# Pairwise attention: the order of scores and transposes, one sequence for two kinds of attention, and a mask on another engine

## What is computed

```
# even layer (block 0), 8 heads: banded, with a sink in the denominator
p = exp(q k / 8 + bias - m)  for keys 0..127 back ; o = p / (sum p + exp(sink - m)) v
# even layer, 8 heads: stick-breaking, strictly causal
z = q k / 8 ;  log_keep = log_sigmoid(-z) where key < query, else 0
a = exp(log_sigmoid(z) + sum of log_keep of later keys) where key < query, else 0 ;  o = a v
# odd layer (block 1), 16 heads: softmax, causal, a bias that stands for three dilated patterns
# block 2, 16 query heads on 4 key heads: softmax over the keys an index has chosen
```

## Time and profile before

| | us |
|---|---|
| median of 3 runs | 3341.68 |
| lowest and highest | 3340.91, 3341.93 |
| the profiled execution | 3343.73 |
| its span in the profile | 3341.9 |

### The profile page before, as it was taken

One profiled execution on the slowest core, in us unless ns is written; L12 is line 12 of the kernel. 1 busy time (PEld: TensorE's weight loads), 2 busy tenths in 40 slices (PEclk: granted clock), 3 DMA queues, 4 the chain that ended last, 5 costly groups with the idle time before them and its releaser, 6 DMA issues.

```text
span 3341.9 us, 36935 instructions
## 1 busy us (share of the span) xinstructions
PE 3184.2 (95%) x14548; PEld 2576.1 (77%) x14548; DVE 1413.5 (42%) x2242; ACT 1188.2 (36%) x1999; POOL 223.0 (7%) x441
## 2 busy tenths in 40 slices
PE   8999995999999999999988999999999998989998
PEld 7888884777788888887866877888887775768887
DVE  3332336554333233323455543332325876443322
ACT  3322326443332132222345533322225636332221
POOL 1000100010000000000310100000042100010000
PEclk9999997999999999999999999999989999989999
DMA  4332220231332323322322412233222230223332
GB/s 142 95 96 100 89 89 1 89 126 51 93 92 93 107 89 95 100 96 83 94 83 70 139 50 87 92 99 101 68 89 76 76 102 19 82 76 95 95 101 70
DMA packets 212606, 291.44 MB, mean 87 GB/s; under 512 B 13873, under 2 KB 135985, under 8 KB 212305
## 3 DMA queue, kind: packets, MB, share of 16 engines
q1 hardware_dynamic: 209792, 279.59, 26.6%
q0 software_dynamic: 2640, 9.50, 0.9%
HBM read 286.94 MB, written 2.10 MB: 86 GB/s over the span
## 4 chain that ended last, share of the span: by engine, by line
PE 86%; DVE 6%; ACT 5%; POOL 1%; issue 1%; DMA 0%; POOLq 0%; DVEq 0%; ACTq 0%
PE ps L94 83%; PE ps L97 3%; DVE sxP L112 1%; DVE ebQ L115 1%; ACT sxP L100 1%; ACT ocP L100 1%; DVE ocP L112 1%; ACT L100 0%; DVE hTl L109 0%; DVE ebP L103 0%; ACT xn L100 0%; POOL stat L103 0%; ACT hTh L100 0%; ACT wh L100 0%; DVE s_ri L115 0%
## 5 line engine op out<-in xcount | busy, mean ns | idle before, releaser
L103 DVE TENSOR_TENSOR wl<-raw,wh 128x1024 fp32r<-128x1024 f32 (+1 forms) x530 | 640.9, 1216 | 1247.5 <-ACT wh L100 1242.6
L100 ACT ACTIVATE wh<-raw 128x1024 fp32r<-128x1024 f32 (+1 forms) x530 | 552.5, 1051 | 1360.0 <-PE ps L94 1316.2
L94 PE MATMUL ps<-hTh,wh 128*128 128x512 f32 x2144 | 839.7, 392 | 16.6 <-DVE hTl L109 16.6
L94 PE MATMUL ps<-hTl,wh 128*128 128x512 f32 x2144 | 837.2, 390 | 0.0
L94 PE MATMUL ps<-hTh,wl 128*128 128x512 f32 x2144 | 837.0, 390 | 0.0
L94 PEld LDWEIGHTS ps<-hTh,wh 128*128 128x128 f32 x2144 | 404.3, 189 | 104.2 <-DVE hTl L109 13.7
L94 PEld LDWEIGHTS ps<-hTl,wh 128*128 128x128 f32 x2144 | 404.2, 189 | 84.9 <-issue 1.0
L94 PEld LDWEIGHTS ps<-hTh,wl 128*128 128x128 f32 x2144 | 404.3, 189 | 84.2
L94 PE MATMUL ps<-wh,hTh 128*128 128x512 f32 (+2 forms) x832 | 324.5, 390 | 10.3 <-DVE hTl L109 5.8
L94 PE MATMUL ps<-wl,hTh 128*128 128x512 f32 (+2 forms) x832 | 321.2, 386 | 0.0
L94 PE MATMUL ps<-wh,hTl 128*128 128x512 f32 (+2 forms) x832 | 321.2, 386 | 0.0
(11 more groups left out here) (344 smaller groups left out, 3918.9 us busy)
## 6 DMA issues: line engine op xcount, KB each, us to landing
raw<-in_ffn_w_gu SPq DMA_DIRECT2D x352, 256.0 KB, 3.1
raw<-in_ffn_w_down SPq DMA_DIRECT2D x88, 512.0 KB, 3.5
raw<-in_xa_w_kv SPq DMA_DIRECT2D x32, 512.0 KB, 3.9
raw<-in_w_in SPq DMA_DIRECT2D x32, 512.0 KB, 3.7
raw<-in_od_w_in SPq DMA_DIRECT2D x24, 512.0 KB, 3.6
raw<-in_w_ffn_gate SPq DMA_DIRECT2D x44, 256.0 KB, 2.9
raw<-in_w_ffn_up SPq DMA_DIRECT2D x44, 256.0 KB, 3.1
raw<-in_w_ffn_down SPq DMA_DIRECT2D x22, 512.0 KB, 3.8
```

Source lines behind the costliest of these rows:

```text
L94: return self.made(lambda e: e.matmul(*a, **k))
L100: return self.made(lambda e: e.activation(*a, **k))
L103: return self.made(lambda e: e.tensor_tensor(*a, **k))
```

## The change

- A `Stage` takes the place of the pairs' tiles: it holds a sequence of pairs that may be of different kinds. The even layer's banded and stick-breaking pairs are one such sequence of eight (`EV`), with no handover and no drain between them.
- Row tiles are five slots, handed to the heads in turn; a head waits for the transposes of the head five before it. The fifth slot is in memory that is free during the stage.
- On PE, the next pair's first two score groups are issued between the transposes of the even and the odd head, and the third group after the odd head's. A banded pair has only two groups, so all its scores go first.
- Stick-breaking: DVE's addition of the mask in the score bank is gone. POOL runs two `affine_select`s for each block after the sigmoids, on the last 128 columns of `P` (fill 0) and of `Q` (fill 1), and DVE's scan waits for `masked`. The `Q` tiles are three, handed to the heads in turn. The scan's second operand is one zero column, broadcast. The memsets are of single columns, and POOL does them before the stage.
- ACT and POOL wait, ahead of the even stage, for tiles of the projection to be free (`even_wait`), and DVE for one ahead of the odd stage; all were used long before.

The diff, cut to its core:

```diff
...
+    class Stage:
+
+
+
+
+        def __init__(self, tag, parts, slots, pt, small, keeps=None):
+            self.tag, self.seq = tag, [(A, s) for A in parts for s in range(A.N)]
+            self.N = len(self.seq)
+            self.p = [(sb(f"{tag}Pa{j}", [P, 512], F32, a), sb(f"{tag}Pb{j}", [P, 768], F32, b))
+                      for j, (a, b) in enumerate(slots)]
             self.pt = [sb(f"{tag}PT{u}", [P, NT, S], F32, pt) for u in range(2)]
             self.sm = [sb(f"{tag}sm{b}", [P, 5, 8], F32, small) for b in range(2)]
...
+        def sbank(self, g, n, u):
+            return 2 * ((self.sfirst[g] + n) % 2) + u
+        def tbank(self, g, u, n):
+            return 4 + (self.tfirst[g] + u * len(self.seq[g][0].groups) + n) % 3
+        def scores(self, g, n, u):
+            A, at = self.seq[g][0], 0
+            for i in A.groups[n]:
+                W = A.spans[i][3]
+                yield i, W, bank[self.sbank(g, n, u)][:, at:at + W]
+        def row(self, g, u, i):
+            pa, pb = self.p[(2 * g + u) % 5]
+            W, o = self.seq[g][0].spans[i][3], (0, 128, 384, 0)[i]
+            return (pa if i == 3 else pb)[:, o:o + W]
+        def keep(self, g, u, i, skip=0):
+            _, _, o, W = CAUSAL[i]
+            return self.q[(2 * g + u) % 3][:, o + i + skip:o + i + skip + W]
+        def slot_wait(self, e, g, u):
+            j = 2 * g + u - 5
+            if j >= 0:
+                e.wait_ge(turned, (self.tag, j // 2, len(self.seq[j // 2][0].groups) - 1, j % 2))
...
-        scores(0)
-        for s in range(A.N + 2):
-            if s >= 2:
-                values(s - 2)
-            if 1 <= s <= A.N:
-                turn(s - 1, 0)
-                turn(s - 1, 1)
-            if s + 1 < A.N:
-                scores(s + 1)
...
+        scores(0, slice(None))
+        for g in range(T_.N + 2):
+            if g >= 2:
+                values(g - 2)
+            if 1 <= g <= T_.N:
+                turn(g - 1, 0)
+            if g + 1 < T_.N:
+                scores(g + 1, slice(0, 2))
+            if 1 <= g <= T_.N:
+                turn(g - 1, 1)
+            if g + 1 < T_.N:
+                scores(g + 1, slice(2, 3))
...
+        def sigmoids(g):
+            A, s = T_.seq[g]
+            act.wait_ge(ones_set, tag)
+            for n in range(len(A.groups)):
+                for u in range(2):
+                    act.wait_ge(scored, (tag, g, n, u))
+                    T_.slot_wait(act, g, u)
+                    j = 2 * g + u - 3
+                    if T_.seq[j // 2][0].stick:
+                        act.wait_ge(normed, (tag, j // 2, j % 2, A.groups[-1][-1]))
+                    for i, W, src in T_.scores(g, n, u):
+                        act.activation(T_.row(g, u, i), src, AF.Sigmoid)
+                        act.activation(T_.keep(g, u, i), src, AF.Sigmoid, scale=-1.0).then_inc(expd, (tag, g, u, i)).also(
+                            drained, (tag, g, "s", n, u))
...
+    def pool_stage(pool, T_):
+
+        tag = T_.tag
+        for g, (A, _) in enumerate(T_.seq):
+            if A.stick:
+                for group in A.groups:
+                    for u in range(2):
+                        for i in group:
+                            W = A.spans[i][3]
+                            pool.wait_ge(expd, (tag, g, u, i))
+                            for t_, fill in ((T_.row(g, u, i), 0.0), (T_.keep(g, u, i), 1.0)):
+                                dg = t_[:, W - P:W]
+                                ins = pool.affine_select(out=dg, in_=dg, compare_op=ALU.is_ge, fill=fill, base=-1,
+                                                         pattern=[[-1, P]], channel_multiplier=1)
+                            ins.then_inc(masked, (tag, g, u, i))
...
-        def before(s):
-
-            dve.wait_ge(const_in, 0)
-            for n, group in enumerate(A.groups):
-                for u in range(2):
-                    dve.wait_ge(scored, (A.tag, s, n, u))
-                    for i, W, src in A.scores(s, n, u):
-                        ins = dve.tensor_tensor(src[:, W - P:W], src[:, W - P:W], mis("strict"), ALU.add)
-                    ins.then_inc(maxed, (A.tag, s, n, u))
...
+        def breaks(g, u):
+            A, _ = T_.seq[g]
             for group in A.groups:
                 for i in group:
                     W = A.spans[i][3]
+                    rev = T_.keep(g, u, i)[:, ::-1]
+                    dve.wait_ge(masked, (tag, g, u, i))
+                    dve.tensor_tensor_scan(rev, rev, T_.zero[:, 0:1].to_broadcast([P, W]), 1.0, ALU.mult, ALU.add).then_inc(step, (tag, g, u, i))
+                    dve.wait_ge(step, (tag, g, u, i))
+                    dve.tensor_tensor(T_.row(g, u, i), T_.row(g, u, i), T_.keep(g, u, i, 1), ALU.mult).then_inc(
+                        normed, (tag, g, u, i))
...
+        def end(g, u):
+            (breaks if T_.seq[g][0].stick else later)(g, u)
+        first(0)
+        for g in range(T_.N + 2):
+            if g < T_.N:
+                end(g, 0)
+            if g >= 2:
+                A, s = T_.seq[g - 2]
+                dve.wait_ge(valued, (tag, g - 2))
+                dve_lo(dve, bank[VBANK][:, :], A.O, A.base + s, slice(0, S)).also(drained, (tag, "o", g - 2))
+            if g + 1 < T_.N and not T_.seq[g + 1][0].stick:
+                first(g + 1)
+            if g < T_.N:
+                end(g, 1)
...
-    def pe_even(pe):
-        pe_pairs(pe, EA, qaT, kaT, lambda s: ("in0", 0, "T", s), lambda c: ("in0", 1, "T", c), lambda s: s // 2,
-                 lambda h, kt: e_tk[:, kt, 128 + 64 * (h // 4):192 + 64 * (h // 4)], [("in0", 1, t) for t in range(NT)])
-        handover(pe, "stick")
-        pe_pairs(pe, EB, qbT, kbT, lambda s: ("qb", s), lambda c: ("kb", c), lambda s: s,
-                 lambda h, kt: e_vb[:, kt, 64 * h:64 * h + 64], [("vb", t) for t in range(NT)])
-
-    def act_even(act):
-        act_pairs(act, EA, hT("out0"), 0, "in0")
-        handover(act, "stick")
-        act_pairs(act, EB, hT("out0"), 4, "in0")
-
-    def dve_even(dve):
-        def bias(h, i, W):
-            dve.wait_ge(table_in, "evb")
-            return evb[:, 256 * (h + 1) - W:256 * (h + 1)]
-        dve_pairs(dve, EA, hT("out0"), 0, bias)
-        handover(dve, "stick")
-        dve_pairs(dve, EB, hT("out0"), 4)
+    def even_wait(e):
+
+        for b in range(2):
+            e.wait_ge(xn_gone, ("in0:1", b))
+        for g in range(2):
+            e.wait_ge(tmp_gone, ("in0", g))
 
     def pool_even(pool):
-        handover(pool, "stick")
-        pool.memset(EB.zr[:, :], 0.0).then_inc(step, "eb zero")
-        for b in range(2):
-            for u in range(2):
-                pool.memset(EB.q[b][u][:, :], 1.0).then_inc(ones_set, "eb")
+        even_wait(pool)
+        pool.memset(EV.zero[:, :], 0.0)
+        for t_ in EV.q:
+            for i, (_, _, o, W) in enumerate(CAUSAL):
+                pool.memset(t_[:, o + i + W:o + i + W + 1], 1.0).then_inc(ones_set, "ev")
+        pool_stage(pool, EV)
...
+    EV = Stage("ev", [EA, EB], [(ev, ev)] * 4 + [(ev_xn, ev)], ev, ev, [ev_gone, ev_gone, ev_xn])
+               [(od, od)] * 4 + [(od_gone, od_gone)], od, od)
+               [(sx_p, sx_p), (sx_p, sx_p), (sx_sc, sx_sc), (sx_xn, sx_xn), (sx_p, sx_xn)], Area(a1 + 16384), sx_p)
...
```

More of the change, by code:

```diff
@@ L746, in row @@
[L746 to L752, removed]
-    VBANK = 7
[L756 to L760, removed]
-            pe.wait_ge(put, kkey(kb))
-            for n, group in enumerate(A.groups):
+            if keeps:
+                self.q = [sb(f"{tag}Q{j}", [P, CAUSAL_W + NT], F32, a) for j, a in enumerate(keeps)]
+                self.zero = sb(f"{tag}Z", [P, 1], F32, small)
@@ new lines, in slot_wait, with pe_stage, scores @@
+        def slot_wait(self, e, g, u):
+            j = 2 * g + u - 5
+            if j >= 0:
+                e.wait_ge(turned, (self.tag, j // 2, len(self.seq[j // 2][0].groups) - 1, j % 2))
+    VBANK = 7
+    def pe_stage(pe, T_):
+        tag = T_.tag
+        def scores(g, part):
+            A, s = T_.seq[g]
+            kb = A.kv_of(s)
+            pe.wait_ge(put, A.qkey(s))
+            pe.wait_ge(put, A.kkey(kb))
+            for n in range(len(A.groups))[part]:
+                group = A.groups[n]
@@ L763, in scores @@
                 for u in range(2):
[L764 removed]
+                    b = T_.sbank(g, n, u)
                     pe.wait_ge(drained, pe.held[b])
[L766 to L768 removed]
+                    pe.held[b] = (tag, g, "s", n, u)
+                for both in zip(T_.scores(g, n, 0), T_.scores(g, n, 1)):
                     for u, (i, W, dst) in enumerate(both):
@@ new lines, in copies @@
+        def copies(g, u):
+            A, _ = T_.seq[g]
+            for n, group in enumerate(A.groups):
+                act.wait_ge(turned, (tag, g, n, u))
+                if g >= 1:
+                    act.wait_ge(valued, (tag, g - 1))
```

(32 more changed lines are left out.)

256 lines of the change are left out of this document (101 added, 155 removed).

## The result

The changed kernel took 3301.07 us (median of 4 runs, 3294.65 to 3303.06) against 3341.8 for the kernel before on the same chip: ratio 0.9874, 95% interval 0.9857 to 0.9892. The forecast was 3303.9, and the time lies in its range. The profiled execution took 3303.06 with a span of 3301.3, 40.6 less than before. The size came out right; two of the reasons did not, and most of what follows is about them.

A forecast was written before the change was run, and what follows sets the result against it. The prediction took the three attention stages to be bound by chains of waits passing between engines. Savings of 21.0 + 8.1 + 8.7 = 37.8 us from the 3341.68 median gave 3303.9, range 3290 to 3317.

The forecast's parts named there:

- The old turn: Softmax stages before: exponentials, first copy, odd head's transposes, next scores and DVE's maxima form a chain of 9.08 us a pair.
- The new period: Softmax stages with scores ahead of odd transposes and a fifth slot: 7.94 us a pair; 8.1 and 8.7 us less.
- two-pair loop through the maxima: Softmax stages: last copy, values, even transposes, scores, maxima (8.4), then ACT's 7.53; 15.9 us for two pairs, the longest loop.
- One sequence: Banded and stick-breaking pairs joined: banded pairs lose 2.0 us, first scan starts at 528.2, 19.4 us earlier.
- The select's price: Stick-breaking part: each POOL select costs DVE 0.15 us, 16 of them 2.4, making 13.2 a pair; bounds 10.8 and 15.4.
- That the tiles come a pair ahead: Stick-breaking part: DVE waits for a tile's second select, but masked tiles are ready a pair ahead.
- rival of a starved POOL: Stick-breaking part: POOL gets in only between DVE's instructions, DVE waits for masks, 15.4 us a pair or more; 3313; chance 0.2.
- DVE as the bound of the stick-breaking part: Stick-breaking part: DVE's scans, products and value remainder take 10.75 us a pair; ACT needs less than DVE.
- rival of free selects: Selects are free, or the loop falls to ACT's own time: 10.8 us a stick-breaking pair; 3292; chance 0.14.
- From the first scan to the value remainder between the last pair's two heads: Stick-breaking part: 49.2 us before, 47.5 after, from three pairs 39.6, one head 6.2, remainder 0.7, about 1 at the start.
- PE order that does nothing: Softmax stages: another wait keeps the loop at 9.08 us a pair; only 21 us gained, 3321; chance 0.09.
- The clock that drops: Softmax stages: denser turns drop PE to half clock, 15 us a pair; slower, 3392; chance 0.04.

The follow-up runs named there:

- e1: Changed kernel with the next pair's scores put back behind both heads' transposes on PE; 3319.4 us, ratio 0.9934.
- e2: Changed kernel with four row-tile slots instead of five, the new PE order kept; 3310.95 us, ratio 0.9909.
- e11: Changed kernel with the even head's exponentials in both softmax stages run over the last 128 columns only; 3298.82 us, ratio 0.9866.
- e12: Changed kernel with the odd head's exponentials shortened in both softmax stages, instead of the even head's; 3293.07 us, ratio 0.985.
- e4: Changed kernel with banded and stick-breaking pairs as two stages again, with a handover between; memsets stay ahead of the stage; 3307.07 us, ratio 0.9895.
- e5: Changed kernel with GpSimd's selects issued in DVE's order of use; 3298.3 us, ratio 0.9869.
- e8: Changed kernel with selects in DVE's order of use and a stick-breaking pair's third score group behind the values on PE; 3299.63 us, ratio 0.9873.
- e9: As e8, but with POOL's selects left out, so the stick-breaking mask is missing; 3296.62 us, ratio 0.9865.
- e10: Changed kernel with the third score group behind the values on PE, GpSimd's select order unchanged; 3302.11 us, ratio 0.9884.
- e3: Changed kernel without POOL's selects, DVE's scans waiting for the sigmoids alone, mask missing; 3299.88 us, ratio 0.9877.

## Why the prediction was right, and where not

- **The old turn** (the first copy's wait, transposes, scores, maxima) was read rightly: e1 brings 9.08 back. The fifth slot was taken for necessary, and e2 shows it.
- **The new period**: 7.94 predicted, 8.03 measured. The step that failed is the one that named the loop. The two-pair loop through the maxima has a duration close to the true one by chance; e11 and e12 exclude it. The prediction listed three loops beside it and left out the one from values through the value half on ACT, although every row of it stood in the trace of before. Its term for ACT alone, 7.53 as before, was low as well: ACT is busy for 7.77 in a turn of the changed kernel. From pair 1 to pair 7 the odd layer took 47.45 where the prediction had 47.25, with two misses against each other: pair 1 to pair 2 took 7.28 (1702.16 to 1709.44), where 7.95 was expected, and the five periods behind it took 40.2, where the sum had 39.3. Half of the latter is a slip in the sum, since five times its own 7.94 is 39.7. So the odd layer's 7.9 less between these pairs agrees with 8.1 by luck in part, and block 2's 8.5 with 8.7. Over the whole stages it is 7.7 and 9.1; of block 2's 9.1 some 0.9 is PE's clock near the end (values 4.54 before and 3.42 after, both behind an idle time of 2.95).
- **One sequence**: the first scan was predicted at 528.2 and came at 528.82, the first sigmoid at 527.08 (near 527 was said). That is partly luck, for this execution began its stage 1.7 earlier, at 494.0. From the stage's start it is 34.8 where the prediction had 32.5, and 2.1 of these 2.3 can be named. The banded pairs (first exponential of pair 0 to that of pair 3) went from 21.42 (499.19 to 520.61) to 20.14 (498.85 to 518.99), 1.3 less, not 2.0. And a table load that nobody had priced came onto the path. ACT's timeline in the kernel before:

```profile
486.07 1.28 ACT L100 ACT_TABLE_LOAD   x1
499.19 0.40 ACT L100 ACTIVATE eaP<-eaP,easm 128x128 f32<-128x128 f32 x1 [11.84 <-DVE easm L106]
```

  and in the changed kernel:

```profile
497.55 1.28 ACT L100 ACT_TABLE_LOAD   x1 [13.21 <-DVE evsm L106]
498.85 0.40 ACT L100 ACTIVATE evPb<-evPb,evsm 128x128 f32<-128x128 f32 x1
```

  The load for the exponentials lay in ACT's idle time and now stands behind its wait for the maxima: from the stage's start the first exponential moved from 3.5 to 4.85. It does so in e4 and e5 too. Why it is issued later, and whether an early dummy activation would hide it, wasn't tried.
- **The select's price**: mis-sized. The prediction had 0.15 for each, 2.4 a pair; they cost 0.65 a pair (11.34 in e8, 10.69 in e9). Its mechanism holds: what a select has left to run when a DVE instruction starts, less 0.14 that is hidden, is what that instruction takes longer, for all scans and products beside selects in the traces of the changed kernel, e5, e8 and e10. The count was wrong. It charged all sixteen as if DVE started together with each; in the earlier trace rows itself the DVE instruction started 0.08 later and took 0.07 longer. In the changed kernel a select waits for a scan or product to end and then runs while the next one starts: a product mostly starts 0.05 before that select's end, which stays hidden, and a scan 0.21 to 0.24 before it, which costs 0.07 to 0.09. So only scans pay, at most one select in two. This case's trace agrees with the Trainium skill (GPSIMD Engine Reference, section 8, Key points) that GpSimd contends with VectorE's instructions that have two SBUF inputs; the amounts are this case's.
- **That the tiles come a pair ahead**: wrong, and it hid the first miss. The second pair's come in a burst, sixteen selects between 540.09 and 547.95 with DVE's first scan at 541.60, and the tile that DVE wants fourth was seventh. Masks cost 1.60, 1.11, 0.67 and 0.67 in the four pairs. The rival of a starved POOL had named this wait, with the wrong cause: its price was 15.4 a pair, and the wait falls from 4.05 (2.92 in e11) to 0.67 with two orders (e8), on GpSimd and on PE, and with as many selects.
- **DVE as the bound of the stick-breaking part**: right for 10.7 of 12 to 12.8. The loop of the third score group and the values at the low clock was not seen; it is why dropping the selects alone (e3) gives no more than 1.0. The rival of free selects, 10.8 a pair, would have been missed for this reason as well: it needs e8's order too.
- **From the first scan to the value remainder between the last pair's two heads**: 47.5 predicted, 44.0 measured (528.82 to 572.86), since the pairs were 12.0 to 12.8 apart rather than 13.2, and the last head's scans were not slowed. With 1.3 less in the tail behind it (9.7 for 11.0) and 2.3 more ahead of the first scan, that makes the 2.4 by which the first stage beat its term.
- **PE order that does nothing**: excluded by e1 (+9.1 and +9.2). **The clock that drops**: excluded. It is 0.93 in both softmax stages with the waits at their ends (0.94 before in the odd layer's), and 1.00 between 1725 and 1749 in the odd layer's, with PE busy for 22.25 of 24.

The best kernel by the stages is e8, 2.3 to 3.8 shorter in the first one than kernels with the changed code. Its run, 3299.63 (3299.09 to 3300.28), can't be told from the changed kernel's 3301.07 (3294.65 to 3303.06).

## What to carry to other kernels

When a wait is taken out of a loop, write down every loop through every buffer that is handed back, the values' bank among them, and test the candidate by shortening the same engine's work inside and outside it, by an amount that is measured and not assumed: a period that moves for one and not for the other names the loop, whereas a changed order can make a loop of its own. When work goes to a helper engine, its total against the period says little; compare the order in which it makes the tiles with the order in which they are wanted, and ask what makes them arrive in a burst. Removing a cost is worth only the distance to the next loop: without the selects the first stage was at most 1.0 shorter, and 3.2 once that loop was gone too. And before a difference between two kernels is read, it is worth knowing by how much the same code varies: here one group of products at one clock or the other, 1.5 us.

## What the runs showed of the hardware

- GpSimd's select of 128x128 in float32 and a DVE scan exclude each other by the instruction. A select that starts inside a scan mostly ends 0.08 to 0.09 after it, so it goes from 0.29 to 1.15 and more (1.21 at most). A DVE instruction that starts inside a select is longer by what the select has left, less 0.14: 0.23 left made scans 0.09 longer, 0.21 left 0.07, and 0.12 (in e5 and e8) or less nothing.
- A scan whose second operand is one broadcast column takes 1.22 for 512 columns, as it did with a full zero tile.
- PE idle for 2.91 was followed by the low clock in e3: the granted clock was 0.50 from 552.15 on, and 16 value products took 4.54 rather than 2.37, just where the chain went through them. That is a cost of a wait beyond the wait itself, but not of every wait: in the changed kernel the same idle time of 2.91 was followed by 1.23 for the score group and 3.41 for the values at 552.47, and by the full clock one pair later. What decides wasn't found. PE's timeline one pair later:

```profile
564.36 0.70 PE L94 MATMUL ps<-e_kbT,e_qbT 64*128 64x256 f32 x4 [2.91 <-ACT evQ L100]
564.99 2.37 PE L94 MATMUL ps<-evPT,e_vb 128*64 128x512 f32 x16
```
